# The last down projection in half-width products: three 512-column products per weight block, or six of 256 columns

## What is computed

```python
D_MODEL = 1024; SEQ = 512
D_FF_2 = 256 * ((8 * D_MODEL // 3 + 255) // 256)     # 2816
# the end of the second layer, x and u both over 512 tokens
u = (gated, convolved projection of x)               # 512 x 2816
x = layer_norm(ALPHA * x + u @ w_down, g, b)         # w_down 2816 x 1024
```

## Time and profile before

| | |
|---|---|
| time, median of 3 runs | 2096.89 us (2096.25 to 2098.32) |
| span of the profiled execution, first to last instruction | 2095.27 us (shown rounded as 2095.3); the median run is 1.6 us longer |
| TensorE busy | 99% of the span, 12912 matmuls and as many weight loads |
| VectorE, ScalarE, GpSimd busy | 43%, 42%, 43% |
| the last down projection | 1958.29 to 2078.9 us of the span |
| what follows it | the final layer norm, to 2095.3 us |

### The profile page before, as it was taken

How to read it: one execution, slowest core, us unless ns; L and a number is a source line. 1 busy time by engine, 2 the same in 40 slices (tenths; PEclk the granted TensorE clock), 3 DMA queues, 4 the chain that set the end, 5 groups by cost and what they waited for, 6 DMA issues and landing times.

```text
span 2095.3 us, 31362 instructions
## 1 busy us (share of the span) xinstructions
PE 2069.4 (99%) x12912; PEld 1681.1 (80%) x12912; DVE 897.6 (43%) x1497; ACT 890.2 (42%) x1678; POOL 896.3 (43%) x690
## 2 busy tenths in 40 slices
PE   9999999999999999999999999999999999999998
PEld 7777778888888888877777888888877788888886
DVE  5331765453510121353337644442257774444222
ACT  4444743453532342254345544442245544444322
POOL 5523320154444445544232544445454264444443
PEclk9999999999999999999999999999999999999999
DMA  7222210142233233222121222233222123222321
GB/s 274 101 79 93 71 38 14 37 151 91 81 100 101 90 101 101 71 91 71 51 71 42 80 96 94 93 101 101 101 71 91 41 81 101 91 92 100 103 99 61
DMA packets 53591, 184.13 MB, mean 88 GB/s; under 512 B 5816, under 2 KB 5824, under 8 KB 53320
## 3 DMA queue, kind: packets, MB, share of 16 engines
q1 hardware_dynamic: 53448, 182.13, 26.1%
HBM read 176.84 MB, written 8.15 MB: 88 GB/s over the span
## 4 chain that ended last, share of the span: by engine, by line
PE 94%; DVE 3%; ACT 1%; issue 1%; POOL 1%; DMA 0%; SPq 0%; POOLq 0%; DVEq 0%; ACTq 0%
PE ps L361 22%; PE ps L363 22%; PE ps L362 22%; PE ps L2826 2%; PE ps L2828 2%; PE ps L2827 2%; PE ps L387 2%; PE ps L381 1%; PE ps L382 1%; PE ps L1167 1%; PE ps L507 1%; PE ps L1169 1%; PE ps L1168 1%; PE ps L479 1%; PE ps L1693 1%
## 5 line engine op out<-in xcount | busy, mean ns | idle before, releaser
L201 POOL TENSOR_TENSOR split_units<-raw_units,split_units 128x512 fp32r<-128x512 f32 x628 | 822.2, 1335 | 1077.5 <-ACT split_units L178 1061.7
L178 ACT ACTIVATE split_units<-raw_units 128x512 fp32r<-128x512 f32 x624 | 356.8, 621 | 353.1 <-PE ps L363 315.3
L361 PE MATMUL ps<-x_split,split_units 128*128 128x512 f32 x1208 | 474.9, 393 | 1.7 <-DVE work L2476 0.8
L363 PE MATMUL ps<-x_split,split_units 128*128 128x512 f32 x1208 | 470.2, 389 | 0.0
L362 PE MATMUL ps<-x_split,split_units 128*128 128x512 f32 x1208 | 470.1, 389 | 0.0
L361 PEld LDWEIGHTS ps<-x_split,split_units 128*128 128x128 f32 x1208 | 226.8, 188 | 54.1 <-issue 4.0
L362 PEld LDWEIGHTS ps<-x_split,split_units 128*128 128x128 f32 x1208 | 226.8, 188 | 47.6 <-issue 1.4
L363 PEld LDWEIGHTS ps<-x_split,split_units 128*128 128x128 f32 x1208 | 226.8, 188 | 47.1
L361 PE MATMUL ps<-hidden_split,split_units 128*128 128x512 f32 x608 | 237.3, 390 | 0.0
L363 PE MATMUL ps<-hidden_split,split_units 128*128 128x512 f32 x608 | 236.6, 389 | 0.0
L362 PE MATMUL ps<-hidden_split,split_units 128*128 128x512 f32 x608 | 236.5, 389 | 0.0
(11 more groups left out here) (538 smaller groups left out, 3264.9 us busy)
## 6 DMA issues: line engine op xcount, KB each, us to landing
raw_units<-stream SPq DMA_DIRECT2D x314, 512.0 KB, 3.3
work<-gate_rows SPq DMA_DIRECT2D x12, 256.0 KB, 2.9
bias_rows<-bias_line SPq DMA_DIRECT2D x1, 2816.0 KB
gate_rows<-work SPq DMA_DIRECT2D x10, 256.0 KB, 2.1
x<-x_t SPq DMA_DIRECT2D x4, 512.0 KB, 6.5
work<-bias_rows SPq DMA_DIRECT2D x1, 2048.0 KB
out_t<-x SPq DMA_DIRECT2D x8, 256.0 KB
vec<-vectors SPq DMA_DIRECT2D x1, 1159.5 KB, 6.0
```

What stands on the lines that cost most here:

```text
L178: scalar.activation(self.split[:, u % SPLIT, 0, part], self.raw[:, u % RING, part], ACT.Copy).then_inc(self.high_done, 1)
L201: gpsimd.tensor_tensor(self.split[:, u % SPLIT, 1, part], self.raw[:, u % RING, part], self.split[:, u % SPLIT, 0, part].bitcast(F32), ALU ...
L361: TE.matmul(out, high, rhs(0, k), start=(k == 0), stop=False)
L363: ins = TE.matmul(out, low, rhs(0, k), start=False, stop=last and shift is None)
```

## The change

In the last down projection alone (`ffn_down_1`), `split_product` is replaced by a new function that takes each weight block through the tokens in two halves: the three matmuls over columns 0 to 255, then the same three over columns 256 to 511. Both halves lie in the same bank. The flag that begins a new sum is set on the first matmul of the bank alone, the one that ends it on the last. The waits for weights and hidden tiles, the release of units and the signal to VectorE are where they were. The other down projection of this kind (`ffn_down_0`) and all other stages keep their products.

```diff
+        def halved_product(pe, out, n_k, rhs, signal, n, ready=None):
+            for k in range(n_k):
+                if ready is not None:
+                    ready(pe, k)
+                high, low = wts.take(pe)
+                last = k == n_k - 1
+                for c in range(2):
+                    now, cols = out[:, 256 * c:256 * c + 256], slice(256 * c, 256 * c + 256)
+                    TE.matmul(now, high, rhs(0, k)[:, cols], start=(k == 0 and c == 0), stop=False,
+                              skip_group_check=True)
+                    TE.matmul(now, high, rhs(1, k)[:, cols], start=False, stop=False, skip_group_check=True)
+                    ins = TE.matmul(now, low, rhs(0, k)[:, cols], start=False, stop=last and c == 1,
+                                    skip_group_check=True)
+                wts.free(ins, signal if last else None, n)
+            ins.then_inc(signal.sem, 1)
@@ stage_linear
+                    if halved:
+                        halved_product(pe, bank(m % 4), n_k, src, tile_ready, m + 1, ready if m == 0 else None)
+                        continue
                     split_product(pe, bank(m % 4), n_k, src, tile_ready, m + 1, ready if m == 0 else None,
                                   shift if m and scaled else None)
@@ steps
-            ("ffn_down_1", lambda: stage_linear(FF2, of(hidden2), "residual", sums="both")),
+            ("ffn_down_1", lambda: stage_linear(FF2, of(hidden2), "residual", sums="both", halved=True)),
```

More of the change, by code:

```diff
@@ L2280, in stage_linear @@
         def stage_linear(n_k, src, mode, out=None, sums=None, before=None, prior=tile_read, scaled=False,
-                         ready=split_ready):
+                         ready=split_ready, halved=False):
             centre = sums == "both"
```

## The result

The changed kernel takes 2104.2 us (median of 5 runs, 2102.86 to 2105.0), the kernel before 2097.4 us beside it (5 runs, 2096.25 to 2098.6). The ratio is 1.0031 with a 95% interval of 1.0020 to 1.0041: it is slower, by 0.3%. The forecast of 2098.7 us, no change, did not come; what came is the first rival, at its upper price.

What follows compares the result with a forecast made beforehand. TensorE, busy 99% of the span, was taken as the bound. 1056 products x 115 ns = 121.4 us, minus 119.7, made 2095.3 us of span 2097.1; plus 1.6 us gave 2098.7 us, range 2096.0 to 2104.0.

Steps and rivals of the forecast that it cites:

- Rival 1: Every start in the stage: 13.3 ns paid per product, 118 to 120 ns pitch, 276 ns matmuls, 2101.8 to 2103.9 us; chance 0.32.
- TensorE bounds the stage and nothing else moves: Last down projection: TensorE always busy, other engines wait behind it; loads, issue, waits, tail and clock costed at nothing.
- The pitch of today, 226.7 ns with 13.3 beside the columns: Last down projection: 512-column fp32r products start 226.7 ns apart, 213.3 for columns; 528 products take 119.7 us.
- The bounds: New 256-column pitch: at least 111 ns by loading alone (117.2 us), at most 120.0 ns with 13.3 fixed (126.7 us).
- the 113 ns between them is what 256 columns of this type stream in: Durations of 389 ns (512 columns) minus 276 ns (256 columns) give 0.441 ns per column, a new pitch of 113.7 ns.
- the term of 115 ns in the sum: New 256-column pitch in the stage: 113.7 ns plus a little over 1 ns for handing over weights; 1.8 us more.
- The pairs of L479: Attention's paired 64-row fp32r products: 0.12, 0.17, 0.23 us at 256, 384, 512 columns, nearly proportional; read as about 118 to 120 ns.
- Rival 2: Stage's weight loads partly exposed: matmuls over 276 ns or starts of 0.13 us and more; a tenth exposed, 2110 us; chance 0.04.
- Rival 3: Stage gains: bare 106.7 ns columns, or repeated weight loads cut short; 7.0 us less, 2089.9 us; chance 0.03.
- The range: Whole kernel time: 2096.0 us (pitch 112.5 ns) up to rival 1's end, 2104.0 us, leaving out rival 2.

Runs made afterwards that it cites:

- the quarters: Changed kernel with each block's products cut into four parts of 128 columns instead of two of 256; 2212.34 us against 2096.82 for the kernel before.

## Why the prediction held in its range and missed in its forecast, point by point

- *TensorE bounds the stage and nothing else moves.* Right, but for the reading that GpSimd was idle half of the time or more: 8.1 busy of 15.0 us is 46% idle. Waits, clock and tail are as forecast, the weight pipeline got slack, and 528 added products cost their pitch and nothing more; doubling them doubled the cost.
- *The pitch of today, 226.7 ns with 13.3 beside the columns.* Right, and it was the number to ask about.
- *The bounds.* The upper one, 106.7 + 13.3 = 120.0 ns, is what was measured, and 1056 x 120.0 - 119.7 = 7.0 us is what the stage became longer by (6.97). The lower one, 111 ns for loading alone, is real too: the quarters run at 111.7. It does not bind at 256 columns.
- *The step that failed: "the 113 ns between them is what 256 columns of this type stream in", and with it the term of 115 ns in the sum.* The 389 ns were of a full product in the stage, the 276 ns of a 64-row pair in the attention. In the stage a 256-column product lasts 283 ns, so the difference is 106 ns, which is 256 columns at 2.4 GHz (106.7) with nothing to spare. The 13.3 ns are paid whole by the 256-column product; they are not halved with its columns. A duration of 276 ns does not tell the pitch either: in the run with 64 weight columns it came with 113 ns, in the pairs of the attention with 118 (below). With 120 in place of 115 the sum would have been 7.0 us. Why fp32r products pay 13.3 ns stays open.
- *The pairs of L479.* The earlier trace rows showed 0.12 us for 256 columns, and I read it down to 118. To the nanosecond, the trace of before has these pairs 118 to 119 ns apart at 256 columns, 169 to 178 at 384 and 231 to 236 at 512. So the pairs do go nearly in proportion to their width; the error was to carry that over to single full products, which are 120.0 and 226.7 ns apart. The 64 rows of each weight block are not the reason: single products with 64 rows ran at 120.0 ns. What makes pairs differ was not tested.
- *Rival 1*, the price per product, had 0.32 and should have had the most. Its size and place came, its duration of 276 ns did not. Rival 2 is out as the cause, though its signs showed: 224 columns with the same load run at 0.11 us and 128 columns at 111.7 ns, so at 256 columns the load is hidden, whatever its traced 192 ns look like. Rival 3 is out.
- *The range.* Its upper end was rival 1's end, 2104.0 us from a median before of 2096.89. The ratio measured, 1.0031, puts the time at 2103.4 on that base, and the later runs' median at 2104.2 on a base of 2097.4. On the first base the range holds by 0.6 us, in the later runs' own times it is passed by 0.2. That it held was luck: it reached that far only to take in the rival, and the mechanism behind the forecast was wrong.

Which version is best: the kernel before. No cut of 512 columns came out below it, and each of its products already fills the 512 columns of its bank. Fewer products, or correct sums made of another type, were not tried.

## What to carry to other kernels

Price a narrower matmul as its columns plus a fixed part per product, with the load's own pace as a floor. From the even streams of this case: the larger of columns / 2.4 GHz + 13.3 ns and 111.7 ns for fp32r with 128 x 128 weights (measured at 512, 256 and 128 columns), and columns / 2.4 GHz + 2.5 ns for bf16. For streams of mixed widths it was off by 1 to 14 ns per block of six products. Take the fixed part from the pitch of the very form that is replaced, and set the forecast by a row with the new width, even a coarse one, before a difference of durations from two forms. A cut in two costs little in bf16 (an estimate of 1.3 us for 528 more products, from 2.5 ns each), five times as much in fp32r, and much more once a part falls below the load's pace.

## What was not expected of the hardware

The fixed part of an fp32r product is 13.3 ns where that of a bf16 product on identities is 2.5 ns, at the same clock in the same stage. And one form, fp32r with 64 weight columns and 256 columns of activations, ran at 113 ns for 30 us and at 120 ns for the rest of the stage, with durations of 276 and 283 ns. What chooses between the two paces was not settled; the full 128 x 128 form was seen only at 120.
